# A two-layer encoder on one core: the input norm's vector moved into the split of the QKV weights, x transposed as it lands

## What is computed

```python
def rmsnorm(x, g):
    y = x * lax.rsqrt(jnp.mean(x * x, axis=-1, keepdims=True) + EPS) * g
...
h = rmsnorm(x, norm_mix[0])
qkv = h @ w_qkv                       # 512 x 1024 @ 1024 x 3072
q = partial_rope(rmsnorm(q, q_gain), cos, sin)      # cos, sin from positions; k likewise
```

## Time and profile before

| | |
|---|---|
| median of 3 runs | 1030.07 us (1029.33 to 1031.6) |
| the profiled execution, its own time | 1029.67 us |
| span in its trace | 1027.9 us |
| TensorE busy | 984.7 us, 96% of the span |
| VectorE busy | 861.0 us, 84% |
| ScalarE, GpSimd busy | 485.0 us and 427.7 us |
| mean granted TensorE clock | 0.990 |

### The profile page before, as it was taken

One profiled execution on the slowest core, in us unless ns is written; L12 is line 12 of the kernel. 1 busy time (PEld: TensorE's weight loads), 2 busy tenths in 40 slices (PEclk: granted clock), 3 DMA queues, 4 the chain that ended last, 5 costly groups with the idle time before them and its releaser, 6 DMA issues.

```text
span 1027.9 us, 12963 instructions
## 1 busy us (share of the span) xinstructions
PE 984.7 (96%) x4724; PEld 807.5 (79%) x4724; DVE 861.0 (84%) x1123; ACT 485.0 (47%) x743; POOL 427.7 (42%) x371
## 2 busy tenths in 40 slices
PE   5999998889899899999999999999999999999998
PEld 4877776666678688888888888898888888888887
DVE  5567889877955999999999987777998999899883
ACT  4525655577745524434345353355443443443520
POOL 5852687565556273664860400252404304124000
PEclk9999999999999999999999999989999999999999
DMA  6423211220123233323332333301333333332202
...
DMA packets 52047, 92.76 MB, mean 90 GB/s; under 512 B 8848, under 2 KB 9872, under 8 KB 51984
## 3 DMA queue, kind: packets, MB, share of 16 engines
q1 hardware_dynamic: 45888, 91.24, 27.9%
q10 hardware_dynamic: 6096, 0.69, 0.5%
...
...
## 4 chain that ended last, share of the span: by engine, by line
PE 76%; DVE 13%; POOL 4%; issue 3%; ACT 2%; DMA 1%; ACTq 1%; SPq 0%; DVEq 0%; POOLq 0%
PE bank L1602 73%; DVE s_nmax L1263 2%; PE bank L1660 2%; DVE s_w_lo L1153 1%; POOL s_o_r L703 1%; DVE s_p L1285 1%; POOL s_oc L706 1%; DVE s_mixc L1283 1%; DVE s_qkn L1215 1%; DVE s_hT_lo L1336 1%; DMA s_raw<-in_attn_w_qkv 1%; DVE s_rt L1219 1%; DVE s_o_ss L1312 1%; DVE s_qk_ss L1202 1%; DVE s_oc L1273 1%
## 5 line engine op out<-in xcount | busy, mean ns | idle before, releaser
L1602 PE MATMUL bank<-s_hT_hi,s_w_hi 128*128 128x512 f32 x512 | 200.8, 392 | 0.0
L1602 PE MATMUL bank<-s_hT_hi,s_w_lo 128*128 128x512 f32 x512 | 199.3, 389 | 0.0
L1602 PE MATMUL bank<-s_hT_lo,s_w_hi 128*128 128x512 f32 x512 | 199.3, 389 | 0.0
L1153 DVE TENSOR_TENSOR s_w_lo<-s_raw,s_w_hi 128x1024 fp32r<-128x1024 f32 x96 | 155.9, 1642 | 13.9 <-ACT s_w_hi L819 7.7
L754 POOL TENSOR_TENSOR s_lt<-s_lbB,s_lbB 128x1024 f32<-128x1024 f32 x14 | 34.1, 2439 | 268.7 <-PE bank L1602 268.2
L1173 DVE TENSOR_TENSOR s_lbB_lo<-s_lbB,s_b_hi 128x1024 fp32r<-128x1024 f32 x64 | 122.6, 1940 | 0.0
L1390 DVE TENSOR_TENSOR s_acc<-s_acc,bank 128x512 f32<-128x512 f32 x168 | 109.3, 681 | 11.0 <-PE bank L1602 10.8
L1602 PE MATMUL bank<-s_b_hi,s_u_hi 128*128 128x512 f32 x288 | 113.2, 393 | 1.9 <-DVE s_a_lo L1378 1.9
L1602 PEld LDWEIGHTS bank<-s_hT_hi,s_w_hi 128*128 128x128 f32 x512 | 96.2, 188 | 20.1 <-issue 0.5
L1602 PEld LDWEIGHTS bank<-s_hT_lo,s_w_hi 128*128 128x128 f32 x512 | 96.2, 188 | 20.0 <-issue 0.5
L1602 PEld LDWEIGHTS bank<-s_hT_hi,s_w_lo 128*128 128x128 f32 x512 | 96.1, 188 | 20.0
...
## 6 DMA issues: line engine op xcount, KB each, us to landing
s_raw<-in_mlp_w SPq DMA_DIRECT2D x64, 512.0 KB, 3.7
s_lbB<-in_mlp_w SPq DMA_DIRECT2D x64, 512.0 KB, 3.3
s_raw<-in_attn_w_qkv SPq DMA_DIRECT2D x24, 512.0 KB, 4.2
s_raw<-in_attn_w_o SPq DMA_DIRECT2D x8, 512.0 KB, 3.2
s_x_nat<-in_x SPq DMA_DIRECT2D x4, 512.0 KB, 8.5
s_x_again<-in_x SPq DMA_DIRECT2D x4, 512.0 KB, 5.0
...
```

The lines of the kernel that those rows point to most:

```text
L1153: v.tensor_tensor(w_lo[slot][:, cols], raw[k][:], f32(w_hi[slot][:, cols]), ALU.subtract)\
L1602: return nc.tensor.matmul(o, lhsT, rhs, start=start, stop=stop, **kw)
```

## The change

- `g_bc` and `hn` go. norm_mix[0] is loaded as columns, `in_col`, 128 partitions by 8 elements of 4 bytes: 1024 separate elements, ahead of `posi` on the same queue.
- TensorE transposes `x_nat` itself, as soon as a tile has landed (`turn_in`). Tiles 0 and 1 are both turned ahead of the first projection.
- The split of slabs 0 to 5 multiplies by the column: each piece, one ScalarE copy of 1024 before, is two scaled copies of 512; each piece's VectorE subtraction of 1024 is two (raw times column, less high) of 512. Both halves of a piece are signalled together. Splits of w_o and of the MLP stay as they were.
- VectorE waits for `in_col` ahead of everything, ScalarE ahead of the first split, behind the first two copies of x.
- The four squares of x move behind the last split of slab 0, ahead of the six small DMA issues.
- TensorE turns the identity into bank 0 18 times at the start and 16 times between x tiles 0 and 1.

```diff
-            act.dma_start(g_bc[:], norm_mix[0].partition_broadcast(P)).then_inc(small_loaded, 16)
+                act.dma_start(in_col[:], norm_mix[0].rearrange("(c p) -> p c", p=P)).then_inc(in_col_loaded, 16)
                 act.dma_start(posi[:], positions.rearrange("a (t p) -> p (a t)", p=P)).then_inc(pos_loaded, 16)
...
             def split_hi(s, k, slot):
                 act.wait_ge(raw_loaded[k], s * 16 + 16)
                 wait_used(act, s - 2)
-                a.activation(w_hi[slot][:, k * PIECE:(k + 1) * PIECE], raw[k][:], ACT.Copy).then_inc(w_hi_done, 1)
+                if s >= WO0:
+                    a.activation(w_hi[slot][:, k * PIECE:(k + 1) * PIECE], raw[k][:], ACT.Copy).then_inc(w_hi_done, 1)
+                    return
+                for c in range(2):
+                    cols = slice(c * BANK, (c + 1) * BANK)
+                    last = a.activation(w_hi[slot][:, k * PIECE + c * BANK:k * PIECE + (c + 1) * BANK], raw[k][:, cols],
+                                        ACT.Copy, scale=in_col[:, 2 * k + c:2 * k + c + 1])
+                last.then_inc(w_hi_done, 1)
...
-            input_squares(0)
             for t in range(NT):
-                split_hi(0, t, 0)
                 h_hi(2 * t)
                 h_hi(2 * t + 1)
-                if t + 1 < NT:
-                    input_squares(t + 1)
+                if t == 0:
+                    act.wait_ge(in_col_loaded, 16)
+                split_hi(0, t, 0)
+            for t in range(NT):
+                input_squares(t)
...
-            def input_gain(t):
-
-                dve.wait_ge(x_loaded[t], 16)
-                if t >= 2:
-                    dve.wait_ge(hn_turned, 2 * (t - 1))
-                v.tensor_tensor(hn[:, t % 2, :], x_nat[:, t, :], g_bc[:], ALU.mult).then_inc(hn_done, 1)
...
             def split_lo(s, k, slot):
                 dve.wait_ge(w_hi_done, s * 4 + (k + 1))
...
+                for c in range(2):
+                    cols = slice(k * PIECE + c * BANK, k * PIECE + (c + 1) * BANK)
+                    last = v.scalar_tensor_tensor(w_lo[slot][:, cols], raw[k][:, c * BANK:(c + 1) * BANK],
+                                                  in_col[:, 2 * k + c:2 * k + c + 1], f32(w_hi[slot][:, cols]),
+                                                  ALU.mult, ALU.subtract)
+                last.then_inc(w_lo_done, 1)
...
-            dve.wait_ge(small_loaded, 16)
-            input_gain(0)
+            dve.wait_ge(in_col_loaded, 16)
             for t in range(NT):
-                split_lo(0, t, 0)
-                if t + 1 < NT:
-                    input_gain(t + 1)
                 h_lo(2 * t)
                 h_lo(2 * t + 1)
+                split_lo(0, t, 0)
...
-            def turn_hn(t):
-                pe.wait_ge(hn_done, t + 1)
+            def turn_in(t):
+                pe.wait_ge(x_loaded[t], 16)
...
+            def keep_turning(n):
+                for _ in range(n):
+                    nc.tensor.transpose(bank[0][:, 0:P], ident[:], ident[:])
+
+            keep_turning(18)
+            turn_in(0)
+            keep_turning(16)
+            turn_in(1)
+            for t, pieces in ((0, (0,)), (1, (0,)), (0, (1,)), (1, (1,)), (2, (0, 1)), (0, (2,)), (1, (2,)), (2, (2,)),
+                              (3, (0, 1, 2)), (0, (3,)), (1, (3,)), (2, (3,)), (3, (3,))):
                 project(t, bank[t], pieces)
-                if (t, pieces[-1]) in ((0, 0), (1, 1), (2, 2)):
-                    turn_hn(t + 1)
+                if (t, pieces) in ((1, (0,)), (1, (1,))):
+                    turn_in(2 + pieces[0])
```

More of the change, by code:

```diff
@@ L294, in build_trunk @@
         probs = [p0, p1]
-        hn, g_bc, x_sq, lam_in, lam_t, ropet = inside(
-            scratch, ("hn", [P, 2, D], F32), ("g_bc", [P, D], F32), ("x_sq", [P, NT, D], F32),
+        x_sq, lam_in, lam_t, ropet = inside(
+            scratch, ("x_sq", [P, NT, D], F32),
             ("lam_in", [P, 4, QK], F32), ("lam_t", [P, 2, QK], F32), ("ropet", [P, 16, NT * HALF], F32))
@@ L311, in build_trunk @@
         gcol = sb("gcol", [P, 4, NC])
+        in_col = sb("in_col", [P, NC])
         qk_col = sb("qk_col", [P, 2])
@@ L358, in build_trunk @@
         r_done = sem("r_done")
-        hn_done = sem("hn_done")
         x_turned = sem("x_turned")
@@ L810, in _ @@
             a = nc.scalar
-            act.dma_start(g_bc[:], norm_mix[0].partition_broadcast(P)).then_inc(small_loaded, 16)
-            with nc.allow_non_contiguous_dma("positions, 2 KB"):
+            with nc.allow_non_contiguous_dma("input gain as columns and positions, a few KB"):
+                act.dma_start(in_col[:], norm_mix[0].rearrange("(c p) -> p c", p=P)).then_inc(in_col_loaded, 16)
                 act.dma_start(posi[:], positions.rearrange("a (t p) -> p (a t)", p=P)).then_inc(pos_loaded, 16)
```

21 lines of the change are left out of this document (10 added, 11 removed).

## The result

The changed kernel takes 1025.23 us (median of 5 runs, 1022.53 to 1025.68) against 1029.92 for the kernel before in the same series (5 runs, 1028.69 to 1031.6). The ratio is 0.995, with a 95% interval of 0.9933 to 0.9967: 0.5% faster. I had forecast 1030.3, no difference, in a range that ended at 1025.6.

A forecast was written before the change was run, and what follows sets the result against it. Slab 2's start was taken as bound by the DMA chain from `posi` to tile 4's copy, with TensorE's front not last. From 1029.67, 0.0 at slab 2 and +0.6 after it gave 1030.3 us, range 1025.6 to 1033.8.

The forecast's parts named there:

- When the columns land: Small loads at the start: each element waits behind one large packet, so `in_col` lands at about 11, `posi` at about 14.
- the forecast's chain: From `posi` at 14 through GpSimd's angles (32.5) and the Sin (32.6) to slab 1 at 38.2 to 38.9, slab 2 at 62.4.
- The first rival: Columns land early, `in_col` at 6.45 and `posi` at 8.5; slab 2 starts 3.8 earlier, 1026.5 us; chance 0.14.
- The angles: GpSimd's work after `posi`: 15.5 us plus about 3 of stretching beside VectorE's three low parts, ending at 32.5.
- The halves' cost behind the Sin: Splits in halves: +0.9 for ScalarE's four splits ahead of tile 0's copy, +0.9 for VectorE's eight low parts before slab 2.
- The attention's 0.6: Slabs 3 to 5: VectorE's low parts in two halves cost 0.3 to 1.4 us, taken as +0.6.
- ScalarE ahead of the Sin: ScalarE is through its last copy of x and the squares by 27, through issues and table load by 31.
- TensorE's front and clock: First matmul at 13.6, slab 0 ends at 37.0 or 38.9 by clock; gains at most 0.5 us, meeting tile 0's copy.
- one of my two cases: TensorE's first matmuls: turning the identity raises the clock, step 0.23 instead of 0.42, and the front ends at 37.0.
- the sentence that I weighed: Transposes do not count as work for TensorE's clock gate; by that rule the front ends at 38.9.

The follow-up runs named there:

- e3: The changed kernel with the positions (`posi`) issued ahead of the columns (`in_col`) on ScalarE's queue; 1030.6 us, ratio to the kernel before 0.9983.
- e5: The changed kernel with `posi` issued from SyncE's queue behind its first eight loads, `in_col` still first on ScalarE's; 1028.91 us, ratio to the kernel before 0.9976.
- e8: The kernel before with splits of slabs 1 to 5 done as in the change, in scaled halves by a column of ones; 1030.28 us, ratio 1.0003.
- e2: The changed kernel without the 34 transposes of the identity; 1026.65 us, ratio to the kernel before 0.9955.
- e1: The changed kernel again, unaltered, for a second profile; 1026.27 us, ratio to the kernel before 0.9949.
- e11: The changed kernel with ScalarE's nine small DMA issues moved ahead of the exponential for lambda; 1020.39 us, ratio to the kernel before 0.9912.

## Why the prediction was wrong, step by step

**When the columns land: the step that failed.** I took the 4.2 us by which `posi` landed behind `g_bc`, spread them over its 512 elements, and charged `in_col` the same price per element though it is first on its queue. `in_col` landed at 4.9 instead of 11, `posi` at 9.9 instead of 14. The number of elements is not what decides: in second place among the large loads 512 of them took 8.5 to 9.3 us and 1024 took 11.4, in first place 1024 took 3.7 to 4.5, without the large loads 2.2 to 2.6. e3 shows columns that land later still (12.7). e5 comes nearest to the forecast's chain: `posi` at 15.5, the Sin at 32.29, slab 1 at 38.09 and slab 2 at 62.51, against the forecast's 14, 32.6, 38.2 and 62.4. In part that is luck, since `posi` was 1.5 later and the angles 1.7 shorter (16.8 against 18.5). And it bears the path out only as far as slab 2: e5 has no wait there, where I had 1.5 to 2.4 (its wait stands at slab 1, 3.91), it starts slab 3 0.8 earlier than before, and it is still 2.5 us faster than the kernel before (1.0 to 3.8), where my sum has no gain. So `posi` alone accounts for about half of the gain; e5's columns landed early. A kernel with both loads as late as I forecast did not run.

**The first rival was the true case.** It gave the first matmul at 10.6 (10.12), slab 0's end at 34 (33.80), slab 2 at 58.6 (56.02) and 1026.5 (1025.23). Its time is nearer than its path: slab 2 came 2.6 earlier than it said. I gave it 0.14, since the trace of before seemed to speak against it; that trace showed only a load in second place. The rule that stood beside it, of whole packets taken from one ring in turn (the Trainium skill, "DMA: Bandwidth & Descriptors", section on queues, rings and completion order), fits the first load's 4.1 us; the second's 8.5 to 11.4 it does not foretell.

**The angles.** I allowed 3 us of stretching by VectorE and reached 18.5 in all; it is 17.2: six small operations were held up, by 0.24 to 0.48 each and 1.9 in sum, where I had three at 1.0. **The halves' cost behind the Sin** was forecast at 0.9 for ScalarE (right: 0.8 in e8, 1.1 after) and 0.9 for VectorE on the chain (wrong: from the copy of tile 0 to that of tile 4 the changed kernel took 1.3 less, 0.5 of it in the nine issues, and its tables were 1.4 shorter). **The attention's 0.6** can't be seen; e8 bounds all of these together between a gain of 0.9 and a cost of 1.6.

**ScalarE ahead of the Sin.** I put its six issues and the table load up to 31. In the trace the issues run from 17.70 on beside its own copies and squares, and the table is loaded by 24.98, 6 us sooner than I had it. Had ScalarE been free at 31 only, it and not the angles would have set the Sin.

**TensorE's front and clock.** Turning the identity raises the clock, as one of my two cases had it, and shows as 0.4 us between the medians of e2 and e1, which is inside the noise. 18 transposes of the identity take 3.9 us (0.22 each), and the 16 after them 1.9 (0.12 each), so the clock had risen under transposes alone, before any product. Here the trace contradicts the sentence that I weighed (the Trainium skill, "TensorE: Matmul & The Clock Gate", Part 4), at least for these float32 transposes of 128x128; that sentence stands beside figures for bf16.

**Where gain is given back.** Of 6.4 us at slab 2, 6.2 are left at slab 3, 7.1 between the two profiled executions and about 5 in the medians, whose runs after the change have the lower clock told above. Before, slab 2 started with a wait of 1.80 and then a stretch of low clock; after, with 0.30 and a high clock, and TensorE runs into a new wait of 1.80 at the first turned q, behind which the granted clock stays at 1.00 (72 to 84 us). From slab 2's start to slab 3's it is 25.7 us before and 25.9 after, in e11 23.7. Both waits belong to the copy of tile 4 and what follows it.

What stays open: why a first small load meets less of the large loads' data than one issued 0.5 us later, and how much of the times beyond slab 3 is due to where waits fall in the attention (e3 kept 1.8 us of gain, 0.1 to 3.4, though its slab 3 started 1.8 later than before; e5 kept 2.5 with its slab 3 only 0.8 earlier).
